# Twelve V buffers in three groups in place of eight in two, with two more k-slices of the query weights read back per tile

## What is computed

```python
h   = layer_norm(x)
mix = concat(window_attention(h), gated_delta_rule(h)) @ w_out
h   = layer_norm(2**0.25 * h + mix)
q   = h @ w_query                       # 8 heads x 2 x 128
s_top, i_top = top_k(q . sub_keys, 16)  # in each half of each head
best, ci = top_k(all sums of the two halves, 16)
expert, gate = i1 * 128 + i2, softmax(best)
act = gelu(expert_u[expert] . h) * gate           # 128 experts a token
h   = layer_norm(2**0.25 * h + sum(act * expert_v[expert]))
```

## Time and profile before

| | |
|---|---|
| median of 3 runs | 3504.99 us (3499.11 to 3507.13) |
| span of the profiled execution (its own time; nothing is recorded around it) | 3777.3 us |
| TensorE busy / VectorE busy / GpSimd busy | 2191.6 / 2151.9 / 2096.8 us |
| row gathers | 2048, 1073.87 MB of 1195.92 MB moved |
| segments with mixing work (4) | 1247 to 2824 us |
| segments without (2) | 2824 to 3569 us |

### The profile page before, as it was taken

The page is one execution under the profiler, slowest core; times in us unless marked ns, Lnnn a source line. Parts: engine busy times, 40 slices in busy tenths (PEclk is TensorE's granted clock), DMA queues, the critical chain, the costliest instruction groups (busy, mean ns, idle before and its releaser), DMA issues. The chain is left out here.

```text
span 3777.3 us, 34501 instructions
## 1 busy us (share of the span) xinstructions
PE 2191.6 (58%) x9905; PEld 1104.5 (29%) x9905; DVE 2151.9 (57%) x6670; ACT 384.3 (10%) x701; POOL 2096.8 (56%) x2079
## 2 busy tenths in 40 slices
PE   6899968747646656635665455556654333333345
PEld 4666655324233233212321232134211000100111
DVE  4333577565667777568656775667666644444300
ACT  2322132111010010001000100010000000000000
POOL 1000056545635566666666657666666766666664
PEclk9999989877767768766766677756776556555676
DMA  8423288877959899989999999999999999999997
GB/s 281 139 66 102 86 276 328 308 266 283 345 184 330 286 336 378 403 325 352 357 403 353 358 335 404 373 341 354 409 344 360 366 362 363 359 373 361 358 363 296
DMA packets 412550, 1195.92 MB, mean 317 GB/s; under 512 B 58993, under 2 KB 135106, under 8 KB 410434
## 3 DMA queue, kind: packets, MB, share of 16 engines
q0 software_dynamic: 294912, 1073.87, 75.6%
q1 hardware_dynamic: 39970, 75.66, 5.6%
q10 hardware_dynamic: 77472, 44.08, 4.1%
HBM read 1172.46 MB, written 21.00 MB: 316 GB/s over the span
## 5 line engine op out<-in xcount | busy, mean ns | idle before, releaser
L998 POOL DMA_INDIRECT U<-in_expert_u,eidx x1024 | 1054.8, 1030 | 575.6 <-issue 287.5
L1380 PE MATMUL bank<-V,ZH 128*32 128x512 f32 x3712 | 726.3, 897 | 915.9 <-DMA V<-in_expert_v,eidxT 727.5
L2159 DVE CUSTOM_DVE_ANT_0 U<-U,h1c 128x512 f32<-128x512 f32 x1368 | 871.8, 690 | 532.6 <-DMA U<-in_expert_u,eidx 393.7
L1006 POOL DMA_INDIRECT V<-in_expert_v,eidxT x832 | 842.7, 1013 | 499.9 <-POOLq L1004 249.2
L1380 PEld LDWEIGHTS bank<-V,ZH 128*32 128x32 f32 x3712 | 142.0, 142 | 1403.9 <-issue 1401.8
L2148 DVE CUSTOM_DVE_ANT_0 U<-U,h1c 128x1024 f32<-128x1024 f32 x256 | 303.2, 1224 | 67.5 <-DMA U<-in_expert_u,eidx 42.7
L310 PE MATMUL bank<-V,U 128*128 128x387 f32 (+2 forms) x928 | 278.4, 459 | 10.6 <-PEq L308 10.5
L1028 POOL COPY eidx<-eidx_n 128x128 uint32<-128x128 uint32 x8 | 3.3, 413 | 413.9 <-POOLq L1027 413.2
L1185 PE MATMUL bank<-wq,arena 128*128 128x512 f32 x400 | 194.1, 634 | 28.7 <-PEq L1308 18.4
L310 PEld LDWEIGHTS bank<-V,U 128*128 128x128 f32 x928 | 178.9, 196 | 100.5 <-issue 21.6
L372 DVE SCALAR_TENSOR_TENSOR U<-bank,U 128x384 f32<-128x384 f32 (+3 forms) x108 | 61.8, 572 | 127.8 <-DVEq L367 117.2
(11 more groups left out here) (308 smaller groups left out, 2834.6 us busy)
## 6 DMA issues: line engine op xcount, KB each, us to landing
arena<-in_w_out SPq DMA_DIRECT2D x56, 512.0 KB
U<-in_w_in ACTq DMA_DIRECT2D x36, 512.0 KB, 3.9
U<-in_expert_u,eidx POOLq DMA_INDIRECT x1024
V<-in_expert_v,eidxT POOLq DMA_INDIRECT x928
raw<-proj_dram SPq DMA_DIRECT2D x8, 1344.0 KB
wq<-in_w_query SPq DMA_DIRECT2D x4, 2048.0 KB, 15.5
proj_dram<-U ACTq DMA_DIRECT2D x35, 192.0 KB, 1.9
arena<-w_dram SPq DMA_DIRECT2D x6, 1024.0 KB
```

The lines of the kernel that those rows point to most:

```text
L998: pool.indirect_dma_start(U[:, c % NU, :], None, expert_u[0], rows(ap=eidx[:, e, c:c + 1], axis=0)).then_inc(g_u[c % NU], 16)
L1006: pool.indirect_dma_start(V[:, c % NV, :], None, expert_v[0], rows(ap=eidxT[:, e, token:token + 1], axis=0)).then_inc(g_v[c % NV // 2], 16)
L1380: last = nc.tensor.matmul(acc_ps[NSTEP * j:NSTEP * j + NSTEP, 512 * n:512 * n + 512], Zb[:, at - i:at - i + NSTEP], buf[j][:, 512 * n:512 ...
L2159: ins = nc.vector.tensor_tensor_reduce(out=U[:, c % NU, lo:lo + D // 2], in0=U[:, c % NU, lo:lo + D // 2], in1=rows[:, lo:lo + D // 2], sc ...
```

## The change

The V ring gets a third group of four buffers. Its room is `wq`'s slices 5 and 6 (two slices of 2048 floats are four rows of 1024), so these are stored to DRAM with slice 7, and from tile 2 on all three are read back per tile, in six transfers, into parts of the arena that the mixing pieces have finished with. Four of them (2.25 MB) are issued where the one (1 MB) was, and two (0.75 MB) after the output weights, behind an additional wait for slice k=5 of these to be used. A fixed table gives the ring group of each of a tile's 32 steps; as 32 isn't a multiple of 3, two groups come back after two steps at the end of a tile. GpSimd's order of rows is unchanged, and so are the U ring, `v_wide` and all arithmetic.

```diff
+MIXED_RING = [i % 3 for i in range(29)] + [0, 1, 2]
+NRING = 3
+LEAN = 3
...
-        w_dram = nc.dram_tensor("w_dram", (P, 2 * PH * P), fp32).ap()
+        w_dram = nc.dram_tensor("w_dram", (P, LEAN, 2 * PH * P), fp32).ap()
...
+                    sp.wait_ge(s_x_free[u], 1)
+                    sp.sem_inc(s_x_free[u], -1)
                     sp.wait_ge(s_h_out[u], 16)
...
-        w_part = view(1024, 2 * PH * P)
+        w_last, w_next = view(1024, 2 * PH * P), [view(4608, 2 * 512), view(7168, 2 * 512)]
+        w_third = [view(3584, 2 * 512), view(6656, 512), view(3072, 512)]
...
+        v_rows = [V[:, 0:4, :], V[:, 4:8, :], wq[:, KD - LEAN:KD - 1, :].rearrange("p k (b d) -> p (k b) d", d=D)]
...
-        g_v = [sem(f"g_v{k}") for k in range(NV // 2)]
+        g_v = [sem(f"g_v{k}") for k in range(2 * NRING)]
...
-        g_vfree = [sem(f"g_vfree{k}") for k in range(NV // 4)]
+        g_vfree = [sem(f"g_vfree{k}") for k in range(NRING)]
...
-                            sp.dma_start(w_part, w_dram[:, :]).then_inc(w_in, 16)
+                            sp.dma_start(w_last, w_dram[:, 2, :]).then_inc(w_in, 16)
+                            sp.dma_start(w_next[0], w_dram[:, 1, 0:1024]).then_inc(w_in, 16)
+                            sp.dma_start(w_next[1], w_dram[:, 1, 1024:2048]).then_inc(w_in, 16)
+                            sp.dma_start(w_third[2], w_dram[:, 0, 1536:2048]).then_inc(w_in, 16)
...
                     sp.dma_start(wo[0], wo_v[KD - 2]).then_inc(b_wo0, 16)
+                    sp.wait_ge(b_wo_free1, 1)
+                    sp.sem_inc(b_wo_free1, -1)
+                    if streamed(t):
+                        sp.dma_start(w_third[0], w_dram[:, 0, 0:1024]).then_inc(w_in, 16)
+                        sp.dma_start(w_third[1], w_dram[:, 0, 1024:1536]).then_inc(w_in, 16)
...
-                def v_row(e, c):
+                def v_row(e, c, ring):
+                    r = ring[c // 4]
                     if c % 4 == 0:
-                        pool.wait_ge(g_vfree[c // 4 % 2], 1)
-                        pool.sem_inc(g_vfree[c // 4 % 2], -1)
+                        pool.wait_ge(g_vfree[r], 1)
+                        pool.sem_inc(g_vfree[r], -1)
                     token = c % 4 * NSTEP + c // 4
-                    pool.indirect_dma_start(V[:, c % NV, :], None, expert_v[0],
-                                            rows(ap=eidxT[:, e, token:token + 1], axis=0)).then_inc(g_v[c % NV // 2], 16)
+                    pool.indirect_dma_start(v_rows[r][:, c % 4, :], None, expert_v[0],
+                                            rows(ap=eidxT[:, e, token:token + 1], axis=0)).then_inc(g_v[2 * r + c % 4 // 2], 16)
...
-                        if k < KD - 3:
+                        if k < KD - 2:
                             last.then_inc((b_wo_free1 if k % 2 else b_wo_free0), 1)
...
-                        pe.wait_ge(w_in, 16)
-                        pe.sem_inc(w_in, -16)
+                        pe.wait_ge(w_in, 16 * 6)
+                        pe.sem_inc(w_in, -16 * 6)
                     for k in range(4 * half, 4 * half + 4):
-                        w = w_part if from_dram and k == KD - 1 else wq[:, k, :]
-                        last = nc.tensor.matmul(o, h1T[:, k, :], w[:, 512 * group:512 * group + 512], start=k == 0, stop=k == KD - 1)
+                        w = w_read(k, group) if from_dram and k >= KD - LEAN else wq[:, k, 512 * group:512 * group + 512]
+                        last = nc.tensor.matmul(o, h1T[:, k, :], w, start=k == 0, stop=k == KD - 1)
...
-                    act.dma_start(w_dram[:, :], wq[:, KD - 1, :]).then_inc(w_stored, 16)
+                    act.dma_start(w_dram[:, :, :], wq[:, KD - LEAN:KD, :]).then_inc(w_stored, 16)
...
+                        if n == 31 and resident:
+                            dve.sem_inc(g_vfree[2], 1)
```

More of the change, by code:

```diff
@@ L132, in pieces, with ring_of @@
     return [n for n in sorted(halves) if halves[n] == half]
+def ring_of(t, i):
+    return MIXED_RING[i]
 def units_beside(n):
@@ L244, in build @@
         s_small = sem("s_small")
-        s_x_free = [sem(f"s_x_free{u}") for u in range(XB)]
         s_tr_free = [sem(f"s_tr_free{u}") for u in range(2)]
@@ L259, in build @@
         gt = sb("gt", [P, 6, T * BH], c=a)
+        s_x_free = [sem(f"s_x_free{u}") for u in range(XB)]
         s_const = sem("s_const")
@@ L726, in build, with w_read @@
         qT = view(1024, 2 * PH, P)
-        w_part = view(1024, 2 * PH * P)
+        w_last, w_next = view(1024, 2 * PH * P), [view(4608, 2 * 512), view(7168, 2 * 512)]
+        w_third = [view(3584, 2 * 512), view(6656, 512), view(3072, 512)]
+        def w_read(k, group):
+            if k == KD - 1:
+                return w_last[:, 512 * group:512 * group + 512]
+            if k == KD - 2:
+                return w_next[group // 2][:, 512 * (group % 2):512 * (group % 2) + 512]
+            if k == KD - 3:
+                return w_third[0][:, 512 * group:512 * group + 512] if group < 2 else w_third[group - 1]
         Lists = namedtuple("Lists", "top itop ftop cand cid best ibest fbest fex den eq first eq_first")
@@ L917, in u_arrived, with v_arrived, wide_arrived @@
             return (t * 16 + 4 + c // NU) * 16 + 16
-        def v_arrived(t, c):
+        first_fills = [4 * (r < 2) + MIXED_RING[NSTEP // 2:].count(r) for r in range(NRING)]
+        tile_fills = [MIXED_RING.count(r) for r in range(NRING)]
+        def v_arrived(t, i):
+            r = ring_of(t, i)
             if isinstance(t, int) and t == 0:
[L922 to L928, removed]
+                return 32 * (4 * (r < 2) + MIXED_RING[NSTEP // 2:i + 1].count(r))
+            return (t * tile_fills[r] + (first_fills[r] - tile_fills[r] + MIXED_RING[:i + 1].count(r))) * 32
+        def wide_arrived(t, i, c):
+            if i % 4 < 2:
+                r = i % 4
+                return 32 * ((first_fills[r] + (T - 2) * tile_fills[r]) * (t > 0) + i // 4 + 1)
             return 16 * ((132 if t > 0 else 16) + c // 16) + 16
@@ L1036, in next_tokens, with mixed @@
                     pool.sem_inc(g_indexfree, 1)
+                def mixed(e, ring):
+                    next_slots(e)
+                    for q in range(P // 4):
+                        for c in range(4 * q, 4 * q + 4):
+                            u_row(e, c)
+                        for c in range(4 * q, 4 * q + 4):
+                            v_row(1 - e, c, ring)
+                        if q == 3:
+                            next_tokens(e)
                 next_slots(0)
@@ L1051, in _ @@
                     u_row(1, 2 * q + 1)
-                    v_row(0, P // 2 + q)
+                    v_row(0, P // 2 + q, MIXED_RING)
                 with pool.Fori(0, T // 2 - 1):
                     for e in range(2):
[L1055 to L1062, removed]
+                        mixed(e, MIXED_RING)
                 for c in range(P):
@@ L1373, in weighted @@
                     in_u = wide and i % 4 >= 2
-                    buf = [(U[:, 4 * (i % 2) + j, :] if in_u else V[:, 4 * (i % 2) + j, :]) for j in range(4)]
+                    r = i % 2 if wide else ring_of(t, i)
+                    buf = [(U[:, 4 * r + j, :] if in_u else v_rows[r][:, j, :]) for j in range(4)]
                     for c in range(4 * i, 4 * i + 4, 1 if in_u else 2):
-                        pe.wait_ge(g_u[c % NU] if in_u else g_v[c % NV // 2], wide_arrived(t, c) if wide else v_arrived(t, c))
+                        pe.wait_ge(g_u[c % NU] if in_u else g_v[2 * r + c % 4 // 2],
+                                   wide_arrived(t, i, c) if wide else v_arrived(t, i))
                     for n in range(2):
@@ L1386, in weighted @@
                             if in_u and n == 1 and j == 1:
-                                last.then_inc(g_ufree[2 * (i % 2)], 1)
+                                last.then_inc(g_ufree[2 * r], 1)
                     if i == NSTEP - 1:
@@ L1391, in weighted @@
                         pe.sem_inc(s_pe, -1)
-                        pe.sem_inc(g_ufree[2 * (i % 2) + 1] if in_u else g_vfree[i % 2], 1)
+                        pe.sem_inc(g_ufree[2 * r + 1] if in_u else g_vfree[r], 1)
                         pe.sem_inc(g_zfree, 1)
@@ L1395, in weighted @@
                     elif in_u:
-                        last.then_inc(g_ufree[2 * (i % 2) + 1], 1)
+                        last.then_inc(g_ufree[2 * r + 1], 1)
                     else:
-                        last.then_inc(g_vfree[i % 2], 1)
+                        last.then_inc(g_vfree[r], 1)
                 def boundary_rows():
```

## The result

The changed kernel takes 3527.10 us (median of 4, 3522.54 to 3535.49), the kernel before on the same chip 3504.72 (median of 4): ratio 1.0070, interval 1.0054 to 1.0085, or 22.4 us slower. I had forecast 3485.

What follows compares the result with a forecast made beforehand. The prediction took the segments to be bound by gathers, with transfers and GpSimd's issue at nearly equal rates. 3505.0 less 46 us saved plus 25.6 us of reads gave 3485 us, own range 3465 to 3498, full range 3410 to 3530.

Steps and rivals of the forecast that it cites:

- A third V group: V ring in the segments: 26 us of plain ring waits plus 20 us of unexplained waits saved, 46 us.
- a stop of GpSimd isn't caught up afterwards: Gathers in the segments: transfer 1.28 us, GpSimd's issue 1.24 us, nearly equal rates, so GpSimd's lost time stays lost.
- Profile and plain runs: Whole kernel: profiled span 3777.3 us against plain median 3505.0; waits without visible cause taken as mostly absent from plain runs.
- the 272 us: Whole kernel: how much longer the profiled span was than the plain median, ascribed to something slow only in the profiled run.
- the 197: GpSimd's V waits without visible cause, 197 us in 67 waits; a tenth, 20 us, counted as saved.
- the 67 late V waits: V waits in the segments whose gather starts 2 to 11 us after TensorE's recorded end; 197 us.
- The reads: Two more k-slices read back per streamed tile, 2.1 MB or 5.1 us each; charged 25.6 us, bounds 0 and 30.8.
- the transfers are the bound and the reads are paid in full; slower: Segments: queue already full, nothing saved, 25.6 to 36 us added, 3531 to 3541 us; chance 0.20.
- SyncE's order, the late weights and the matmuls at nothing: SyncE's queue and routing matmuls: extra bytes hidden by 24 and over 50 us of cover, matmuls same 592 ns; cost nothing.
- The store: One bigger store issued at 622.0, 3.1 MB for 1.0; at most 5.1 us of queue time, taken as 0.
- The wait only moves to the U ring: U ring in the segments: GpSimd waits there instead, saving equals cost, 3498 to 3512 us; chance 0.22.
- the second rival: Segments: transfers are the bound and reads are paid in full, 3531 to 3541 us; chance 0.20.

Runs made afterwards that it cites:

- e19: Changed kernel with three V groups but only slice 7 stored and read back, on kind A: 3499.39 us against 3500.97 for the kernel before, 0.9995.
- e8: The kernel before, unchanged, run again for a second profile on a chip of kind B: 3770.55 us, ratio 1.0021.
- e16: Changed kernel with the V ring back at two groups, all six reads kept, against the kernel before on kind B: ratio 1.0034.
- e5: The whole change, unchanged, against the kernel before on a chip of kind B: ratio 1.0265.

## Why the prediction was wrong

**The step that failed** is the saving of 46 us in "A third V group", and beneath it the sentence "a stop of GpSimd isn't caught up afterwards". That sentence sets one gather against one issue, 1.28 us against 1.24, and leaves out what else the queue moves. The rows of the kernel before had it: 360 GB/s over 1577 us is 568 MB, 1388 us at 409 GB/s, and GpSimd's own 1032 rows at 1.30 us are 1342. With the late signals away the transfers bind, and a stop of GpSimd costs nothing: the ring alone saved 1.6 us (e19).

"Profile and plain runs" came close and missed this. "I treat most of them as absent from the plain run" was right for kind A as far as its traces show, but I took the 272 us for something of the profiled execution, still counted 20 us of the 197 and 26 of the other waits as a saving, and didn't ask what binds a tile that is 28 us shorter. The profile showed a chip on which V groups come free late after TensorE's recorded work, the times fit one where they don't. This is, for each V wait of GpSimd over 0.6 us from 1250 us on, the start of the gather against the recorded end of the weighted step that frees its group (worked out from the instruction records; the counts are waits, the rest us):

```
                              V waits  over 1.6 after the end  median  longest
profiled kernel before           85              72              6.8     11.4
e8  kernel before, B             92              76              6.8     12.5
e16 reads only, B               104              84              5.6     11.6
e5  the change, B                33              29             14.4     22.5
the change, A                    11               0              0.8      0.8
e19 ring only, A                 10               0              0.8      0.8
```

The Trainium skill (Perfetto Trace Analysis, "Per-instruction lifecycle") says that the shown end of a TensorE instruction is computed. On kind A all 21 gathers follow it by 0.8 us, so there it fits. On kind B the row is free later; whether the work itself ends late or only its signal, the records don't tell. So the 67 late V waits were real where they were recorded. The kernel before wasn't profiled on kind A, so what its V waits are there isn't known.

**The saving, forecast 46 us, measured 0** (e19, 1.6 us). What the engines wait for shows why. VectorE's and TensorE's longest waits in the four segments, in the changed kernel on kind A:

```profile
DVE U L2203 <- DMA U<-in_expert_u,eidx: 275.1, 121, 10.0
DVE actT L2235 <- DVEq L2234: 22.2, 4, 7.3
...
PE bank L1422 <- DMA V<-in_expert_v,eidxT: 337.1, 67, 12.5
PE bank L1422 <- DMA wq<-in_expert_v,eidxT: 160.3, 34, 9.0
PE bank L1396 <- PEq L1395: 34.1, 4, 13.7
...
PE bank L1126 <- PEq L1123: 13.5, 16, 0.8
```

and on kind B (e5):

```profile
DVE U L2203 <- DMA U<-in_expert_u,eidx: 65.7, 27, 8.3
...
DVE arena L1837 <- DVEq L1836: 49.0, 7, 12.4
DVE raw L1859 <- DVEq L1858: 40.1, 7, 15.5
...
PE bank L1422 <- issue: 97.5, 26, 8.8
PE bank L1422 <- DMA wq<-in_expert_v,eidxT: 93.9, 14, 9.3
PE bank L1396 <- PEq L1395: 77.3, 4, 21.8
PE bank L1126 <- PEq L1123: 71.9, 14, 18.8
PE bank L1422 <- DMA V<-in_expert_v,eidxT: 70.3, 19, 7.0
```

On kind A both wait mostly for rows: TensorE 497 us, and 105 at its own queue's waits, most of which are for other engines' signals. On kind B it is the other way round, 164 and 316 us, and VectorE's wait for rows falls from 275 to 66 us. Where they wait for rows, GpSimd's stops are an effect of the transfers: 396 GB/s over 1454.6 us is 576 MB, of which 1032 gathers are 541. At 409 GB/s the 576 take 1408 us, and GpSimd's own 1032 x 1.30 us only 1342. "A stop of GpSimd isn't caught up afterwards" fails there: the other 35 MB, 86 us at 409 GB/s, are time in which it catches up.

**The reads, forecast 25.6 us, measured 22.4 to 26** on kind A, by the whole change and by the subtraction above, 4.8 us a tile for the 5.1 of the sum. The rival "the transfers are the bound and the reads are paid in full; slower" is what happened, within 4 us of its lower end. I named the point from which it decides, a plain segment below about 352 us. By the profile of e19 (three groups, one read) the four segments are 353 to 368, above that point, and the last two are 337 and 329, the ceiling of 330 that I gave. So the reads were paid in full from a little above the point that I named. By the rule of the Trainium skill that I set beside it (DMA: Bandwidth & Descriptors, "Where 436 GB/s comes from"), 358 GB/s would bind; the trace disagrees, with 409 GB/s held for 200 us (3100 to 3300), so the rival was right by its mechanism and not by that figure.

**SyncE's order, the late weights and the matmuls at nothing** were right: 28 and 54 us of cover, 592 ns. The store took 15.1 us to land; what it costs no run shows, and it is within the 26 us above.

**On a chip of the kind whose profile I read** the forecast would have failed otherwise. "The wait only moves to the U ring" is what happens, and more than the wait. GpSimd's waits over the four segments with two groups (e16) and with three (e5), on two chips of kind B:

```profile
POOL V L1043 <- POOLq L1041: 196.9, 70, 10.6
POOL U L1034 <- POOLq L1033: 79.5, 25, 11.6
```

```profile
POOL U L1034 <- POOLq L1033: 253.3, 51, 14.3
...
POOL V L1043 <- POOLq L1041: 56.6, 23, 5.5
POOL wq L1043 <- POOLq L1041: 18.4, 4, 4.9
```

V falls by 122 us, U rises by 174. Shown for kind B: it is the depth, not the reads, the place or the experts, and most of it is lost in steps 0 to 15. Not shown: why. GpSimd's order is the same with more freedom, so something must come later for it; the handshakes of mixing pieces between TensorE and VectorE are what grew. That TensorE's late signals, which only the traces of kind B have, turn depth into loss fits all runs, and no run took them away. The granted clock differs too: in the four segments of the changed kernel it is 0.71 on kind B (e5) and 0.75 on kind A, and TensorE is busy 924 us against 846 with VectorE at 1046 and 1047. Whether that is a cause of the loss or follows from the waits no run tells. It stays open.

No run beats the kernel before by a measurable amount on either kind of chip. That the measured 22 us lie near the 25.6 charged for the reads is the second rival's merit; the forecast's own sum had the sign wrong.

## What to carry to other kernels

Before a difference between a profile and a time is explained, look at the profiled execution's own time and at unprofiled ones from the same chip. Here, wherever both are on record, they agree with the span within 1%; a span that is far from the time then points to another chip, and its waits may not exist where the time was taken. A ring that is full is a symptom until one knows what its consumers wait for: if it is rows from memory, a deeper ring gave nothing here and the bytes that made room for it were paid. Where they wait for each other's signals, the wait moved to the next ring.

## What the runs showed of the hardware

- Two kinds of chips (or lasting states of a chip), 3501 to 3505 and 3764 to 3803 us for one kernel, about 8% apart (one chip of kind B gave 3803 in one comparison and 3767 in another); kernels compare differently on them (the ring alone 0.9995 and 1.023 to 1.028).
- On kind B the V groups come free late, 72 of 85 waits over 1.6 us after TensorE's recorded end in the profiled kernel before, none of 21 on kind A. Where semaphore events can be paired with TensorE's instructions, none is over 0.5 us late in the first 463 us of three traces of kind B (the profiled kernel before, e8, e5). Traces of kind B hold fewer events of the engines' semaphores for the same kernel (10644 in e5, 13588 for the change on kind A), so a share of late signals would be of the recorded ones alone. What holds them wasn't found.
- The rate stops at about 409 GB/s (409 over 3100 to 3300 us on kind A, 412 in the fastest window of 30 us, e5), with reads, gathers and other transfers together, in both kinds.
